# Latent queries made pair by pair in the first attention, and the join of two attention kinds on four groups of partitions

## The reference

```python
# layer 0, samples: latent attention over the cache
q_lat  = jnp.einsum("bthn,chn->bthc", q_nope, w_uk)
s_past = jnp.einsum("bthc,bkc->bhtk", q_lat, ckv_past) + jnp.einsum("bthr,bkr->bhtk", q_pe, kpe_past)
s_new  = jnp.einsum("bthc,bkc->bhtk", q_lat, c_kv) + jnp.einsum("bthr,bkr->bhtk", q_pe, k_pe)
p = softmax(concat(s_past, s_new) * scale)
# layer 1, prompt: three dilated groups, joined by maximum and denominator
M   = reduce(jnp.maximum, [m for _, m, _ in parts])
num = sum(o * jnp.exp(m - M)[..., None] for o, m, _ in parts)
den = sum(dn * jnp.exp(m - M) for _, m, dn in parts)
return num / den[..., None]
```

## Time and profile before

| | us |
|---|---|
| median of 3 runs | 1707.36 (1706.73 to 1708.23) |
| the profiled execution, whole | 1708.9 |
| its span | 1707.1 |

### The profile page before, as it was taken

How to read it: one execution, slowest core, us unless ns; L and a number is a source line. 1 busy time by engine, 2 the same in 40 slices (tenths; PEclk the granted TensorE clock), 3 DMA queues, 4 the chain that set the end, 5 groups by cost and what they waited for, 6 DMA issues and landing times.

```text
span 1707.1 us, 28106 instructions
## 1 busy us (share of the span) xinstructions
PE 1524.9 (89%) x12031; PEld 1401.0 (82%) x12031; DVE 701.7 (41%) x993; ACT 471.9 (28%) x882; POOL 610.8 (36%) x276
## 2 busy tenths in 40 slices
PE   6868887688799999999999979998859999999998
PEld 6756555355599989998999979997629989999898
DVE  4767751788345310242112475215556430034112
ACT  4224442334233211122221111104613221122221
POOL 2311103244236643465433432321012663356441
PEclk9989986699899999999999999988959999999999
DMA  4267305377233534444344555437911353543421
GB/s 145 70 219 249 124 1 179 125 291 294 99 124 125 196 125 146 141 178 148 124 148 149 169 184 174 143 137 247 316 54 50 124 197 127 194 144 127 148 75 50
DMA packets 123370, 258.53 MB, mean 151 GB/s; under 512 B 7136, under 2 KB 104560, under 8 KB 116944
## 3 DMA queue, kind: packets, MB, share of 16 engines
q1 hardware_dynamic: 117136, 219.49, 37.6%
q0 software_dynamic: 6144, 37.75, 5.9%
HBM read 249.62 MB, written 95.58 MB: 202 GB/s over the span
## 4 chain that ended last, share of the span: by engine, by line
PE 80%; DVE 10%; ACT 3%; issue 3%; DMA 2%; POOL 1%; SPq 0%; POOLq 0%; DVEq 0%; ACTq 0%
PE ps L501 21%; PE ps L505 20%; PE ps L502 20%; PE ps L760 4%; PE ps L667 2%; DVE sq L1584 1%; PE ps L704 1%; PE ps L898 1%; ACT sc L2082 1%; PE ps L861 1%; PE ps L678 1%; PE ps L779 1%; PE ps L1001 1%; PE ps L733 1%; DVE KT L1452 1%
## 5 line engine op out<-in xcount | busy, mean ns | idle before, releaser
L2129 POOL TENSOR_TENSOR whl<-wraw,whl 128x2048 fp32r<-128x2048 f32 (+3 forms) x127 | 446.4, 3523 | 603.1 <-ACT whl L1794 603.1
L501 PE MATMUL ps<-hA,whl 128*128 128x260 f32 x1248 | 335.6, 289 | 19.3 <-POOL hA L2129 13.9
L502 PE MATMUL ps<-hA,whl 128*128 128x260 f32 x1248 | 330.8, 286 | 0.0
L1794 ACT ACTIVATE whl<-wraw 128x2048 fp32r<-128x2048 f32 (+3 forms) x127 | 185.9, 1484 | 481.2 <-PE ps L505 397.1
L501 PE MATMUL ps<-uT,whl 128*128 128x260 f32 x1024 | 273.6, 288 | 16.8 <-POOL uT L2129 16.8
L502 PE MATMUL ps<-uT,whl 128*128 128x260 f32 x1024 | 270.8, 285 | 0.0
L501 PEld LDWEIGHTS ps<-hA,whl 128*128 128x128 f32 x1248 | 240.2, 193 | 21.4 <-POOL hA L2129 15.6
L505 PE MATMUL ps<-hA,whl 128*128 128x260 f32 x1248 | 255.2, 286 | 0.0
L502 PEld LDWEIGHTS ps<-hA,whl 128*128 128x128 f32 x1248 | 240.6, 193 | 0.1
L501 PEld LDWEIGHTS ps<-uT,whl 128*128 128x128 f32 x1024 | 196.8, 192 | 17.6 <-issue 17.6
L505 PE MATMUL ps<-uT,whl 128*128 128x260 f32 x1024 | 209.7, 287 | 0.0
(11 more groups left out here) (290 smaller groups left out, 2032.1 us busy)
## 6 DMA issues: line engine op xcount, KB each, us to landing
out_ds<-in_state SPq DMA_DIRECT2D x32, 2047.0 KB, 10.5
wraw<-in_w_up SPq DMA_DIRECT2D x32, 1024.0 KB, 5.6
wraw<-in_w_down SPq DMA_DIRECT2D x32, 1024.0 KB, 5.1
wraw<-in_w_qkv SPq DMA_DIRECT2D x18, 1024.0 KB, 6.2
out_ds<-in_state SPq DMA_DIRECT2D x8, 2044.0 KB, 12.8
dv<-in_state SPq DMA_DIRECT2D x36, 256.0 KB, 5.9
dv<-q_scratch SPq DMA_DIRECT2D x6, 1024.0 KB, 6.8
wraw<-in_w_omla SPq DMA_DIRECT2D x4, 1024.0 KB, 5.1
```

The lines of the kernel that those rows point to most:

```text
L501: pe.matmul(ps[:, 2 * u + a, 0:HALF], hi(k), rhs(k, 0)[:, c], start=first, stop=False)
L502: pe.matmul(ps[:, 2 * u + a, 0:HALF], hi(k), rhs(k, 1)[:, c], start=False, stop=False)
L1794: ins = act.activation(dst(0), src, ACT.Copy)
L2129: return pool.tensor_tensor(dst, src, hi.bitcast(F32), ALU.subtract)
```

## The change

Two places are rewritten.

First, the latent queries. `wukT` is gone; SP loads 64 x 512 of it for each pair into `sq` (two slots, `load_wuk`), and for pairs from the third on waits until PE has used the slot. PE makes a pair's latent queries in `latent_queries`, 4 matmuls of 8 columns into the last 128 columns of banks 6 and 7: those of the first pair in step 0, those of the next pair in step 3 of each pair. The key product of `project` is cut into two halves of 256 columns, so that it leaves these columns free. `rotate` frees the unit after its second product. The new token's products, its scores (into bank 5), the copies to `qrep` and the mask are spread over the last steps, and two cache groups are gathered two pairs earlier. At the end of the attention DVE clears `qbd` and turns group 0 ahead of the last output product and group 1 behind it.

Second, the join. The statistics are turned so that the four token tiles lie on partitions 0, 32, 64 and 96 upwards (`turn_stats`), 8 heads in each: the maxima inside the last unit after its first `d_turn`, the sums after its last. The shares are worked out on 128 x 128, and spread by 16 matmuls with 256 columns, each from one group of 8 partitions into a bank of its own, in two halves. Far outputs are put into token order when they leave `ps`. The samples' output moves into units 3 to 5. Each joined tile is released by itself, and the output product waits for tile after tile.

```diff
-                    free(rotate(u, qh[64:96, h % 4, :]))
-                    dve.wait_ge(tile_taken, vw.at("tile_summed"))
-                    link(dve.tensor_copy(qS[:, h, :], qh[:, h % 4, 0:NS]))
+                    link(rotate(u, qh[64:96, h % 4, :], free_link))
+                    dve.tensor_copy(qS[:, h, :], qh[:, h % 4, 0:NS]).then_inc(queries_kept, 1)
...
+            def latent_queries(p):
+
+                pe.wait_ge(wuk_in[p % 2], 16 * (p // 2 + 1))
+                pe.wait_ge(queries_kept, 2 * (p + 1))
+                for k in range(2):
+                    for a in range(2):
+                        h = 2 * p + a
+                        ins = pe.matmul(ps[:, 6 + k, LQ + h * NS:LQ + (h + 1) * NS], wuk_pair(p)[:, a, k * P:(k + 1) * P],
+                                        qS[0:NOPE, h, :], start=True, stop=True, skip_group_check=True)
+                ins.then_inc(query_latents, 1)
...
+                if n == 0:
+                    latent_queries(0)
+                if n == NI + 2:
+                    pe.wait_ge(tile_taken, vw.at("tile_summed"))
...
+                if t == 3 and n < NI - NB_T:
+                    pe.wait_ge(tile_taken, vw.at("tile_summed"))
+                    latent_queries(p + 1)
+                if n == NI - 1:
+                    new_scores()
...
+            def load_wuk(p):
+
+                if p >= 2:
+                    sp.wait_ge(query_latents, p - 1)
+                sp.dma_start(wuk_pair(p), io["w_ukT"].rearrange("p (h c) -> p h c", h=H)[:, 2 * p:2 * p + 2, :]).then_inc(
+                    wuk_in[p % 2], 16)
...
+                    load_wuk(0)
+                if j:
+                    load_wuk(j)
                 copy_some(2)
...
-            sp.wait_ge(output_ready, H // 2)
-            sp.dma_start(wukT, io["w_ukT"].rearrange("p (h c) -> p h c", h=H)).then_inc(wuk_in, 16)
...
                     dve.wait_ge(output_ready, p)
+                    if n >= NI:
+                        for i in range(2):
+                            ins = dve.memset(qbd[i][:], 0.0)
+                        ins.then_inc(queries_cleared, 1)
+                        turn_group(0)
...
+                if n == NI - 3:
+                    new_products_out()
+                if NI - 2 <= n < NI + 2:
+                    copy_queries(n - (NI - 2))
+                if n == NI:
+                    new_bias()
...
+                if p == H // 2 - 3:
+                    pool.wait_ge(tile_summed, mark["projected"])
+                    gather(0)
+                    gather(1)
...
+            def turn_stats(n, src):
+
+                for t in range(NB_T):
+                    pe.matmul(ps[32 * t:32 * t + GH, 2 * n, 0:P], src[:, 0, t, :], ident[:], start=True, stop=True, skip_group_check=True)
+                for b in range(NB_T):
+                    for t in range(NB_T):
+                        r = slice(32 * t, 32 * t + 32)
+                        ins = pe.matmul(ps[32 * t:32 * t + GH, 2 * n + 1, b:P:NB_T], src[r, 1, b, :], ident[r, r], start=True, stop=True,
+                                        skip_group_check=True)
+                ins.then_inc(stats_turned, 1)
...
+            for i in range(2):
+                if i:
+                    pe.wait_ge(dil_out_taken, DU)
+                for p in (2 * i, 2 * i + 1):
                     for t in range(NB_T):
+                        r = slice(32 * t, 32 * t + GH)
+                        ins = pe.matmul(ps[:, 4 * i + t, (p % 2) * 2 * P:(p % 2 + 1) * 2 * P], spread[r, p * P:(p + 1) * P], share[r, :, :],
+                                        start=True, stop=True, skip_group_check=True)
...
-            split_ready(4)
             for c in range(2):
-                linear(4, 4, 2 * MC, hA_k)
+                linear(4, 4, 2 * MC, hA_k, ready=None if c else first, units=range(4))
```

More of the change, by code:

```diff
@@ L516, in linear @@
                 for mt in range(m_tiles):
-                    u = z_begin()
+                    u = z_begin(units[mt] if units else None)
                     c = slice(mt * P, (mt + 1) * P)
-                    ins = whole(u, lambda k: hi[:, k, c], lambda k: lo[:, k, c], rhs, range(nk))
+                    ins = whole(u, lambda k: hi[:, k, c], lambda k: lo[:, k, c], rhs, range(nk),
+                                ready=ready if mt == 0 else None)
                     z_end(ins)
@@ new lines, in shares @@
+            def shares():
+                dve.wait_ge(shares_exp, 1)
+                dve.wait_ge(stats_turned, 2)
+                dve.tensor_tensor(whole_den, share[:, 0, :], ps[:, 2, 0:P], ALU.mult)
+                link(dve.tensor_tensor(far_den, share[:, 1, :], ps[:, 3, 0:P], ALU.mult))
+                link(dve.tensor_tensor(whole_den, whole_den, far_den, ALU.add))
+                link(dve.reciprocal(peak, whole_den))
+                for kind in range(2):
+                    ins = dve.tensor_tensor(share[:, kind, :], share[:, kind, :], peak, ALU.mult)
+                ins.then_inc(shares_ready, 1)
@@ new lines, in _ @@
+            for k in range(DU + 2):
+                if k < DU:
+                    d_max(k)
+                if k == DU + 1:
+                    shares()
+                if k >= 2:
+                    d_out(k - 2)
+                if k in (3, 4):
+                    sample_out(k - 3)
+                if k == 5:
+                    for f in range(4):
+                        dve.tensor_copy(tmp[:, (a0 + f) % 4, 0:NS], oSd[:, f, :])
+                if k == DU:
+                    share_exponents()
@@ L2099, in _ @@
                     d_taken(k, j)
[L2100 to L2101 removed]
+                    if k == DU - 1 and j == 2:
+                        share_exp()
             for f in range(4):
```

259 lines of the change are left out of this document (129 added, 130 removed).

## The result

| | before | after |
|---|---|---|
| median | 1707.05 us (1704.61 to 1708.23, 4 runs) | **1647.23 us** (1646.42 to 1653.67, 4 runs) |
| ratio | | 0.9662, 95% interval 0.9645 to 0.9678 |
| span of the profiled execution | 1707.1 | 1651.8 |

The kernel is faster, by 57.7 us going by the ratio. 1655.4 was forecast: the direction and the range held, the size was 6 to 8 us short. Two more groups of runs, each with its own runs of before beside it, gave the unaltered changed kernel 0.9654 (0.9627 to 0.968) and 0.967 (0.964 to 0.97).

What follows compares the result with a forecast made beforehand. TensorE held 80% of the chain of waits, but two stretches away from dense work counted: between layer 0's attentions and layer 1's join. -31.5 and -20.5 gave -52, so 1707.4 became 1655.4 us; range 1644 to 1674.

Steps and rivals of the forecast that it cites:

- 1a: Layer 0, between prompt and sample attention: first `unit_scores` 7.5 us after the last `values` instead of 35.8, -28.3 us.
- 1b: Prompt attention: releasing the projection unit before DVE's add shortens ten PE waits by 0.71 us each, -7.1 us.
- 1c: Latent queries taken into the prompt attention: 2.1 us over seven pairs, 1.3 first pair, 0.5 last pair; together +3.9 us.
- The last pair: Prompt attention's last pair: new scores and ACT's copies cost 0.5 us, at most 3.06.
- Units 0 and 1: First sample-attention units, at half clock before: left unchanged, though 6 us more if both ran at full clock.
- part 1: Everything up to the sample attention, with stretch, early release, added attention work and SP queue: -31.5 us.
- 1d: SP's load list in the attention: weight chunks asked for one pair later still land, margin about 2 us, cost 0.
- Rival (c): Sample attention starts early, then waits for cache gathers from group 3: 1 us once, about 5 if repeated, 1660; chance 0.08.
- The join: Layer 1, last unit's values to first output tile: 1263.0 against 1284.98, -22.0 us; -20.5 after a +1.5 clock allowance.
- The spreading: Join, shares spread by sixteen matmuls in two halves: 3.5 us a half at full clock, 7.0 at half clock.
- (b): Join packs and clock holds: spreading 2.0 us a half, second tile and first cache units at full speed, 1646; chance 0.12.
- slow second tile: Join's output product: PE waits between quarters and may run the second tile, 2.9 us, at half clock, +1.5 us.

Runs made afterwards that it cites:

- join-only kernel: The new join with the old latent queries, against the kernel before the change: 1681.98 us, ratio 0.9843.
- the kernel with the far product in PSUM: Changed kernel, but the second of a joined tile's three operations writes to PSUM and the add reads it there: 1649.05 us, ratio 0.9635 of the kernel before.

## Why the prediction was right, and where it was off

**The stretch between the attentions (1a)** was right to the tenth: V + 7.6 against V + 7.5, -28.2 against -28.3. The gap between the two attentions was made of DVE's and ACT's lists as worked out.

**The loop (1b, 1c)** was right. A pair was to change by -0.71 + 0.3, and did by -0.40; undoing the release gave +0.72, and doubling the queries showed that a pair has no more than 0.6 us to hide them in. At step 28 the offset is -3.3; by the terms it was to be -7.1 + 2.1 + 1.3 = -3.7.

**The last pair** is a term that was mis-sized: +0.5 was allowed, and +2.9 came (35.3 against 32.3). Not the new scores or ACT's copies did it, as the bound had it, for with the clock up the pair takes 29.1 us with them in place; it was the granted clock, which fell to 0.50 at 256. Before, it was 0.50 from 248 to 256 and 0.97 from 256 to 264. I had read the clock only at units 0 and 1 and in the join.

**Units 0 and 1** gave 1.3 us each (5.75 and 5.82 against the 7.06 of the earlier trace rows). I had left them as they were. That the smaller idle time raised the clock is not shown: unit 0 took 6.9 to 7.0 us behind 6.5 us of idle PE in the three profiles with the new queries on the first group's chip, and 5.64 behind 11.19 in the join-only kernel. With the last pair the two misses cancel, which is luck: part 1 was put at -31.5, the traces have -31.2, and alone on the chip it gave 32.8.

**The SP queue (1d)** cost nothing: no wait of ACT for DMA at a chunk's split in the attention. **Rival (c)** was there with 0.66 us, once, at the fifth group and not at the fourth that it named.

**The join** was put at -22.0 for the first output tile and gave -25.6. The step that failed is the price of TensorE's small work there: the time at which the shares are ready, and the spreading behind them.

The shares were put 15.2 us behind the last maximum (1248.4 against 1233.2) and came 10.4 behind it. Three things make the 4.8:
- The turn of the statistics at 2.9 us (20 matmuls in 40 passes, where before there were 8 in 8 passes; so two and a half times as many matmuls and five times the passes). Its two parts take 0.33 and 0.41, 0.75 together, so 2.15 too much in the second. The row that I took as nearest, 0.058 us for a matmul into a quarter of the partitions, was five times too slow for 32 columns: 0.011 us each. Below the lower end of 2.3, too.
- The first turn at 1.1 us on the path. It is hidden whole in PE's wait of the earlier trace rows.
- Four groups of turns and values between them, 4.2 us. The code was read rightly, four groups of the same passes stand there; the clock was not. In the earlier trace rows they ran at a granted clock of 0.50, in the changed kernel at 1.00, and took 2.4.

The clock over them in the kernel before (its first group is in the earlier trace rows), then PE's timeline of the first two groups and their clock in the changed kernel, and the kernel with the far product in PSUM, in which the same code took the 4.2 us again (1207.91 to 1212.11):

```profile
1238.00:1242.00 4.00, 3.99 (x24) 2.88 (x24) 0.00 (x0) 1.04 (x2) 0.00 (x0) 0.50 1.21 502
```

```profile
1209.19 0.66 PE L1007 MATMUL ps<-scT,dv 128*64 128x128 f32 x8 [1.50 <-ACT scT L2191]
1209.78 0.66 PE L993 MATMUL ps<-ident,sc 128*128 128x128 f32 x4
...
1208.00:1212.00 4.00, 2.81 (x49) 1.91 (x52) 0.34 (x2) 2.87 (x9) 0.00 (x0) 1.00 1.36 550
```

```profile
1207.91 1.12 PE L1007 MATMUL ps<-scT,dv 128*64 128x128 f32 x8 [1.40 <-ACT scT L2191]
...
1208.00:1212.00 4.00, 4.00 (x24) 2.79 (x24) 0.00 (x0) 1.24 (x3) 0.00 (x0) 0.50 1.24 485
```

So this third part, 1.8 us, is the clock's and not the change's: of the twelve profiles with the new join, five have the shares 10.4 us behind the last maximum and seven 12.0 to 12.8. From these 5.1 the shares themselves take 0.3 back (2.5 instead of 2.2).

The spreading was priced by its columns, 7.0 us a half at half clock and 3.5 at full. In the changed kernel's profile both halves took 3.66 together, nearly all of it at a granted clock of 0.50; a second profile of the same kernel has it at 1.00:

```profile
1216.00:1220.00 4.00, 2.58 (x26) 1.86 (x20) 2.99 (x5) 0.64 (x1) 0.27 (x1) 0.50 0.00 0
```

```profile
1206.53 2.04 PE L1047 MATMUL ps<-sq,rope 8*128 8x256 f32 x32 [1.61 <-DVE sq L1818]
```

That is about a quarter of the price at either clock (14.00 and 7.0), for the same columns: the four groups of rows work side by side. Since DVE starts on the first half, only 1.5 us of it came out of the path (2.0 instead of 3.5). Against that, three of four adds took 1.35 instead of 0.69, which no term had (+2.0), and PE's last quarter of the first output tile ran at half clock (1.7 instead of 1.0). The joining was to take 11.1 us from the first tile on and took 13.6.

Of the rivals, (b) was the nearer: 1646 against a measured 1647 to 1651. But its reasons held only in part. Turns and spreading pack better than it said (it had 2.0 us a half, and 1.0 came at the full clock), while the clock was 0.50 from 1216 to 1232 as the forecast's slow second tile had it, and units 0 and 1 were not at full speed.

## What to carry to other kernels

When latency-bound work is moved into another loop, price it by the wait that is already there and try it by doubling the moved part; here a pair hid 0.6 us and not more. Where the engine clock can fall to half, read its row in every stretch that the sum runs through, those that a price is taken from included, and don't lean on one profile for it: the same code ran at either level, and a price taken at 0.50 was charged to work that ran at 1.00. When matmuls are laid on other groups of rows, don't price them by their columns alone. Before filling a gap to speed up what follows it, look what that meets next: with the first units at full speed the gathers were late, by as much as had been won.

## What the runs showed of the hardware that I had not expected

- 32x32 turns with four partition groups alternating took 0.41 us for 32 passes, some 0.011 us from start to start, all into one PSUM bank. Group by group it was 0.77, 0.024 each. The Trainium skill, TensorEngine Tiling (Array Packing), "Restrictions and Gotchas", has it that different row tiles cannot access one bank at the same time; these traces show no price of that, though they don't show in which cycle each one writes. The same page, "Instruction Overhead", gives each matmul some 60 cycles, by estimate 0.025 us at 2.4 GHz. With a pass taken for a matmul, the row in group order agrees, the alternating one is below half of it.
- Spreading 8192 columns in passes from 8 rows each took 14.00 us from one group of rows and 3.66 from four groups of rows into four banks, both at a granted clock of 0.50; at 1.00 the four groups took 2.04 (unaltered kernel, second profile). The order of the groups changed little (3.79).
- VectorE's add with both operands and the result in SBUF took 0.69 us alone and 1.34 to 1.38 beside POOL's split, in each of the nine profiles with the new join and without the edit; with one operand in PSUM it took 0.69 beside the same split. The multiplications by a PSUM operand (0.67 to 0.69) were never slowed. In the changed kernel's rows above, the split runs from 1219.73 to 1221.05 and the add that began at 1220.21 ends at 1221.59, 0.54 behind the split: it looks held back and not slowed. The Trainium skill, SBUF — State Buffer, "Who interferes with whom", states such an exclusive lock between a VectorE instruction with two SBUF inputs and a GpSimd instruction that reads SBUF; the trace agrees, and I had left it out of the sum.
- A product of two plain 128x128 operands is two passes of 0.115 us at full clock; a transpose of the same size is one (the four of a group at L993 are x4 in the rows above).
- TensorE's granted clock went either way for the same instructions, from one execution to another. The last attention pair took 33.3 to 36.4 us in six profiles of seven and 29.1 in one; with 24 idle products spread over the pair it was 0.71 to 0.79 from 256 to 264 and 0.85 to 1.00 behind, and three profiles of three had 27.9 to 29.7 us.
